# Broadcasting rows with matmuls over all 128 rows of the array

## The reference, cut to what matters

```python
# forgetting attention (8 heads, layer 0 of the first block)
logits = q_b @ k.T * scale + F_b[..., :, None] - F[..., None, :]      # F = cumsum(log_f)
# mLSTM (4 heads, layer 1 of the first block)
D = b[..., :, None] - b[..., None, :] + i[..., None, :]               # decay, then exp
# head norms (second block, both layers), per head of 64 or 32 features
q_gqa = rms_norm_2(q_g.reshape(b, l, GQA_HEADS, GQA_DIM), lp["g_qn_gqa"])
```

## Time and profile before

| | us |
|---|---|
| median of 3 runs | 2605.84 (2600.36 to 2607.82) |
| the profiled execution, its own time | 2602.29 |
| its span | 2600.5 |
| PE busy (matmul records) | 2534.8 (97%) |
| VectorE busy | 1263.5 (49%) |
| ScalarE busy | 534.0 (21%) |
| GpSimd busy | 641.8 (25%) |
| mean granted TensorE clock | 0.983 of full speed |

### The profile page before, as it was taken

The page is one execution under the profiler, slowest core; times in us unless marked ns, Lnnn a source line. Parts: engine busy times, 40 slices in busy tenths (PEclk is TensorE's granted clock), DMA queues, the critical chain, the costliest instruction groups (busy, mean ns, idle before and its releaser), DMA issues.

```text
span 2600.5 us, 36667 instructions
## 1 busy us (share of the span) xinstructions
PE 2534.8 (97%) x14020; PEld 2055.5 (79%) x14020; DVE 1263.5 (49%) x2507; ACT 534.0 (21%) x1167; POOL 641.8 (25%) x523
## 2 busy tenths in 40 slices
PE   8999999999999999999999999999999999999999
PEld 5857889986699998645567767888888865899999
DVE  3024168751325886314646763544552235335774
ACT  1131122111212221212530002222200124212220
POOL 0010134200212530001422321332340004332562
PEclk9989999999899999998999999999999998999999
DMA  6322255644234566110023571222212220243442
GB/s 239 130 97 89 106 208 189 255 174 161 83 130 164 197 230 231 70 59 25 1 81 146 215 270 65 75 88 97 98 68 77 98 83 1 98 171 142 165 179 106
DMA packets 39826, 335.31 MB, mean 129 GB/s; under 512 B 3856, under 2 KB 10128, under 8 KB 22416
## 3 DMA queue, kind: packets, MB, share of 16 engines
q1 hardware_dynamic: 39696, 333.50, 34.6%
HBM read 332.44 MB, written 1.05 MB: 128 GB/s over the span
## 4 chain that ended last, share of the span: by engine, by line
PE 87%; DVE 5%; DMA 3%; issue 2%; POOL 2%; ACT 1%; DVEq 0%; SPq 0%; POOLq 0%; ACTq 0%
PE PS L757 23%; PE PS L557 20%; PE PS L2674 6%; PE PS L1509 5%; PE PS L1019 5%; PE PS L1692 4%; PE PS L1327 3%; PE PS L2715 3%; PE PS L1680 2%; DMA slot<-in_weights 2%; PE PS L2250 2%; PE PS L1338 2%; PE PS L1350 2%; PE PS L432 1%; PE PS L2367 1%
## 5 line engine op out<-in xcount | busy, mean ns | idle before, releaser
L557 PE MATMUL PS<-XN,slot 128*128 128x256 f32 (+1 forms) x1184 | 296.8, 411 | 0.8 <-DVE XN L496 0.8
L757 PE MATMUL PS<-SQ,slot 128*128 128x128 f32 (+1 forms) x1984 | 294.4, 301 | 2.4 <-DVE slot L853 2.4
L757 PEld LDWEIGHTS PS<-SQ,slot 128*128 128x128 f32 x1984 | 268.1, 191 | 15.6 <-DVE slot L853 2.7
L557 PEld LDWEIGHTS PS<-XN,slot 128*128 128x128 f32 x1184 | 224.4, 190 | 69.9 <-issue 42.5
L757 PE MATMUL PS<-XN,slot 128*128 128x128 f32 (+1 forms) x1664 | 250.0, 301 | 0.0
L557 PE MATMUL PS<-arena,slot 128*128 128x256 f32 x1088 | 238.4, 381 | 9.6 <-DMA slot<-in_weights 9.6
L557 PEld LDWEIGHTS PS<-arena,slot 128*128 128x128 f32 x1088 | 208.0, 191 | 38.5 <-issue 9.8
L757 PEld LDWEIGHTS PS<-XN,slot 128*128 128x128 f32 x1664 | 226.1, 192 | 10.7
L880 DVE SCALAR_TENSOR_TENSOR arena<-PS,small,arena 128x255 f32<-128x255 f32 (+2 forms) x352 | 174.8, 543 | 45.9 <-ACT arena L824 45.6
L824 ACT ACTIVATE arena<-PS,small 128x256 f32<-128x256 f32 (+1 forms) x176 | 105.3, 616 | 379.1 <-DVE PS L913 240.4
L1468 POOL TENSOR_SCALAR probs<-probs,pair_rec 128x512 f32<-128x512 f32 (+2 forms) x64 | 88.2, 1383 | 247.7 <-DVE pair_rec L1436 247.7
(11 more groups left out here) (280 smaller groups left out, 3806.0 us busy)
## 6 DMA issues: line engine op xcount, KB each, us to landing
slot<-in_weights SPq DMA_DIRECT2D x85, 2048.0 KB, 7.7
arena<-in_mod SPq DMA_DIRECT2D x96, 512.0 KB, 3.4
slot<-in_weights SPq DMA_DIRECT2D x16, 2816.0 KB, 9.8
slot<-in_weights SPq DMA_DIRECT2D x24, 1536.0 KB, 6.8
slot<-in_weights SPq DMA_DIRECT2D x6, 1024.0 KB, 4.8
slot<-in_weights SPq DMA_DIRECT2D x2, 2176.0 KB, 8.9
arena<-in_c SPq DMA_DIRECT2D x3, 1024.0 KB, 10.4
small<-in_small SPq DMA_DIRECT2D x1, 2685.0 KB, 18.6
```

Of the source, the lines that this page charges most:

```text
L557: mm = pe.matmul(o, l, r, start=k == 0, stop=k == len(terms) - 1, skip_group_check=True)
L757: mm = pe.matmul(PS[:, bank, 0:h], lhs[:, k * P:(k + 1) * P], rhs(k), start=first and k == 0, stop=last and k == 3, skip_group_check=True)
```

## The change

1. `select` now gives one column of the whole 128 x 128 identity, broadcast to as many columns as wanted, and the moving side is all 128 partitions of the row's area (`row_of`). Only the wanted partition meets a 1; the other 127 meet zeros and must only hold finite numbers.
2. In the mLSTM layer a GpSimd memset clears the 128 x 256 area first, and DVE waits for it before it writes the decay rows.
3. A spread of the head norms is 2 matmuls (heads of 64) or 4 (heads of 32), each with 128 rows and 64 or 32 columns of the array, written to its own PSUM partitions. 17 matmuls a layer become 42. The two 0/1 tables leave the table `small` (768 of its columns).
4. Layer 1 of the second block sets 2 x 32 partitions of the unused half of PSUM bank 7 to 1.0 with DVE, and the statistics' matmuls wait for it.

```diff
-        def select(n, h):
+        def select(h, each=P):
-            return ident[0:n, h:h + 1].broadcast_to([n, P])
+            return ident[:, h:h + 1].broadcast_to([P, each])
+        row_of = lambda r: arena[:, 14336 + r * T:14336 + r * T + T]
...
-                        sc.append((i, c0, c1, select(8, 2 * t + i), rows[0:8, 0, 0:c1 - c0], False, True))
+                        sc.append((i, c0, c1, select(2 * t + i), row_of(0)[:, 0:c1 - c0], False, True))
...
-                    dec.append((c0, c1, select(4, h), rows[0:4, 2, 0:n], True, True))
+                    dec.append((c0, c1, select(h), row_of(2)[:, 0:n], True, True))
...
-                add(tensor=tensor_lstm_gates, vector=vector_lstm_gates)
+                add(tensor=tensor_lstm_gates, vector=vector_lstm_gates,
+                    gpsimd=lambda p: p.memset(row_of(2), 0.0).then_inc(*tick(GD, "lstm", "cleared")))
...
                     dve.wait_ge(*of("lstm", "F"))
+                    dve.wait_ge(*of("lstm", "cleared"))
...
+                if nq < 512:
+                    for g in (1, 2):
+                        op = dve.memset(PS[32 * g:32 * g + 32, 7, nq:512], 1.0)
+                    op.then_inc(*tick(VD, hn, "unused_set"))
...
                 claim(pe, STAT)
+                if nq < 512:
+                    pe.wait_ge(*of(hn, "unused_set"))
...
-                lhs, r = sel_rows(name, t)
+                g, _, _, _, heads, _, _, _ = tiles[name, t]
+                each = P // heads
                 claim(pe, bank)
                 pe.wait_ge(*of(hn, "rstd"))
-                pe.matmul(PS[:, bank, 0:n], lhs, RST[r, 0:n], start=True, stop=True)\
-                    .then_inc(*tick(TD, hn, "spread", name, t))
+                for i in range(heads):
+                    mm = pe.matmul(PS[each * i:each * (i + 1), bank, 0:n], select(32 * g + heads * t + i, each), RST[:, 0:n],
+                                   start=True, stop=True, skip_group_check=True)
+                mm.then_inc(*tick(TD, hn, "spread", name, t))
```

More of the change, by code:

```diff
@@ L165, in small_columns @@
     sizes["stat"] = 2
-    sizes["spread_halves"] = 4 * P
-    sizes["spread_quarters"] = 2 * P
     sizes["rope_mla"] = 2 * T
@@ L2387, in scalar_low, with vector_low @@
                     act.activation(q_sq[h], q_dst[h], ACT.Square).then_inc(*tick(SD, hn, "sq", "Q", h))
-            def vector_low(dve, s=s, nq=nq, q_dst=q_dst):
+            def vector_low(dve, s=s, l=l, nq=nq, q_dst=q_dst, hn=hn):
+                if nq < 512:
+                    for g in (1, 2):
+                        op = dve.memset(PS[32 * g:32 * g + 32, 7, nq:512], 1.0)
+                    op.then_inc(*tick(VD, hn, "unused_set"))
                 for m in range(0, 4, 2):
@@ L2416, in two_blocks, with tensor_stat @@
                     stat_groups[g].insert(0, (pick("all", 1), SQ_KR, 512, (f"kv{l}", "read", 2, 0)))
-            def tensor_stat(pe, hn=hn, stat_groups=stat_groups):
+            def tensor_stat(pe, hn=hn, stat_groups=stat_groups, nq=nq):
                 claim(pe, STAT)
+                if nq < 512:
+                    pe.wait_ge(*of(hn, "unused_set"))
                 for i in range(7):
@@ L2470, in two_blocks, with tensor_spread @@
             SIN = [SQ[:, 4 + i, 0:T] for i in range(4)]
[L2472 to L2477, removed]
+            def tensor_spread(pe, name, t, hn=hn, tiles=tiles, bank_of=bank_of):
                 bank = bank_of["S", name, t]
                 n = tiles[name, t][3]
-                lhs, r = sel_rows(name, t)
+                g, _, _, _, heads, _, _, _ = tiles[name, t]
+                each = P // heads
                 claim(pe, bank)
                 pe.wait_ge(*of(hn, "rstd"))
-                pe.matmul(PS[:, bank, 0:n], lhs, RST[r, 0:n], start=True, stop=True)\
-                    .then_inc(*tick(TD, hn, "spread", name, t))
+                for i in range(heads):
+                    mm = pe.matmul(PS[each * i:each * (i + 1), bank, 0:n], select(32 * g + heads * t + i, each), RST[:, 0:n],
+                                   start=True, stop=True, skip_group_check=True)
+                mm.then_inc(*tick(TD, hn, "spread", name, t))
                 lend(bank, (hn, "out", name, t))
@@ L3140, in small_array @@
     put("stat", stat)
-    r, c = i[:, None] % 32, np.arange(4 * P)[None]
-    put("spread_halves", (c // 64 == r) * 1.0)
-    put("spread_quarters", (c[:, :2 * P] // 32 == r) * 1.0)
     i = np.arange(P)
```

## The result

The changed kernel takes **2581.5 us** (median of 4 runs, 2580.5 to 2584.2), the kernel before on the same chip 2606.8 us (4 runs, 2600.4 to 2607.9). The ratio is 0.991, 95% interval 0.9891 to 0.9928: by it the kernel is some 23 us or 0.9% faster (the two medians lie 25.3 us apart). The profiled execution took 2581.9 us (span 2580.1, mean granted clock 0.996), that of before 2602.3 (2600.5, 0.983).

The account below looks back on a forecast made before the run. It took PE's own time, columns and clock, as the bound. Gains 7.7 + 5.9 + 0.3 + 10.4 = 24.3 us bring the profiled 2602.3 to 2578.0; with 3.5 added, median 2581.5 us, range 2572 to 2602.

Parts of the forecast that it names:

- What lets the clock fall: All four places, 71 us at 0.50: matmuls using 4 or 8 rows count little for the clock, full ones count.
- Rival A: All places: clock ignores rows used and falls in the same places; 10.7 us slower, 2616.5 us; chance 8%.
- C: Both head norms: clock kept only where no wait stands before, so it still falls there; 2 us gained, 2604; chance 7%.
- D: One of the four places: clock still falls there, 6 to 10 us of gain missing, 2589 in the middle; chance 14%.
- Forgetting attention: Forgetting attention: 2.75 us a unit, unit 4 starting 13.2 us after unit 0's start instead of 20.9; gain 7.7 us.
- mLSTM: mLSTM layer: four units 7.8 us instead of 12.1, gain 4.3; the records behind them gain 1.6; together 5.9 us.
- Layer 0: Layer 0 head norms: spreads stage 27.5 us instead of 21.8, loss 5.7; scores gain 3.9, Fourier records 2.1; net gain 0.3.
- the change of parting: Switching how the array is parted: 0.1 us a change, ends zero and 0.2; 12 changes, 1.2 us, in each head-norm layer.
- Layer 1: Layer 1 head norms: spreads stage 15.1 us instead of 20.0, gain 4.9; scores 3.9, Fourier records 1.6; gain 10.4 us.
- Memsets and table: mLSTM and layer 1 memsets, and the table smaller by 393 KB: zero effect, at most about 1 us.
- rival B: Head norms: column parts of a spread run one after another; 12.5 us slower, 2618.3 us; chance 3%.
- 3.5 us: Whole run: median of the runs shown lies this far above the profiled execution, so 2578.0 becomes a median of 2581.5 us.

Follow-up runs that it names:

- e5_rows72: Kernel before, with the row-broadcasting matmuls of forgetting attention and mLSTM on 72 of 128 rows, head norms unchanged: 2599.1 us, one run.
- e6_rows32: Kernel before, with the row-broadcasting matmuls of forgetting attention and mLSTM on all 32 rows of a strip, head norms unchanged: 2598.4 us, one run.
- e9_first3r8: Changed kernel, but the first three sets of spreads in both head norms side by side with 8 rows: 2578.9 us, ratio 0.9904 to before.
- e3_spreads: Kernel before, with only the new head-norm spreads on 128 rows in both layers, tables kept: 2596.8 us, ratio 0.997 to before.
- e4_side32: Changed kernel, but head-norm spreads side by side as before, with all 32 rows of their strips: 2585.4 us, ratio 0.9915 to before.
- e1_fox: Kernel before, with only the forgetting attention's selecting matmuls on 128 rows: 2597.2 us, ratio 0.9964 to before.
- e8_first3: Changed kernel, but the first three sets of spreads in both head norms side by side in 32-row strips: 2577.4 us, ratio 0.9897 to before.
- e12_last3: Changed kernel, but the last three sets of spreads in both head norms side by side in 32-row strips: 2591.5 us, ratio 0.9949 to before.
- e2_lstm: Kernel before, with only the mLSTM decay matmuls on 128 rows, plus memset and DVE's wait: 2601.3 us, ratio 0.9984 to before.

## Why the prediction was right, point by point

The forecast was that the clock, not the columns, is what the change buys, and that all four stretches at 0.50 go. They did. By its own terms:

- **What lets the clock fall.** Forecast: few rows count little. Shown, by e5_rows72, e6_rows32 and e9_first3r8, with the addition that the neighbours' rows count with them. In e5_rows72 PE is busy 19.50 of 19.50 us and stays at 0.50, and the change of rows alone takes the stretch away. The rule that the Trainium skill gives in "TensorE: Matmul & The Clock Gate", Part 1 (how busy PE has been) has no place for rows, and the traces do not agree with it. Rival A is out. So are C and D: layer 1's spreads start behind a wait of 1.25 us and stay at 1.00.
- **Forgetting attention**, 7.7 us: measured 7.8; the unit is 2.75 us as priced. The 2.83 us that I read for the old unit "at full clock" hold 0.2 us at half: the clock fell at 160.7, before the last selecting record was through. In e3_spreads, where it fell later, the old unit takes 2.74. The wait of 0.4 to 0.8 us for the probabilities is 0.24.
- **mLSTM**, 4.3 + 1.6: measured 3.7 + 1.6. I had priced a unit at 1.35 us of PE and 0.81 of wait for DVE. The starts stand 2.28 to 2.36 apart, so PE's part is 1.5, but 1.38 in the last unit, behind which PE does not wait. I read the difference of some 0.15 us as the end of the last record, which a next one hides only when PE need not wait; no run tests this.
- **Layer 0**, loss 5.7, gain 6.0: measured 6.7 and 5.9. The mis-sized term is the change of parting. The 17 spreads took 15.8 us, 1.2 more than 17 x 0.86, and the records beside them are longer too: seven rotations took 3.6 us where I had 3.0, three Fourier steps 8.2 where I had 7.8. That is 2.1 us in all over the 12 changes that I had counted, so 0.18 for one in place of 0.1, within the ends that I gave (zero and 0.2). I had also counted too few: the first two sets, which mix spreads of two and of four parts, take 0.27 us more than their columns, the next three 0.14. The part beside the spreads shows in the rows: four Fourier records take 0.97 us to the next start behind a set of spreads (1189.06 to 1190.03), and 0.86 behind rotations (1196.12 to 1196.98), which also have 128 rows and 128 columns.

```profile
1189.06 1.13 PE L2517 MATMUL PS<-small,arena 128*128 128x256 f32 x4
1190.03 1.89 PE L2528 MATMUL PS<-small,arena 128*128 128x256 f32 x8
...
1196.12 1.03 PE L2517 MATMUL PS<-small,arena 128*128 128x256 f32 x4
1196.98 1.89 PE L2528 MATMUL PS<-small,arena 128*128 128x256 f32 x8
```

  At the end of layer 0's spreads I had DVE's last product; it is POOL's rotation (0.90 us of wait), of nearly the same length.
- **Layer 1**, 4.9 + 3.9 + 1.6: measured 3.8 + 5.4. The changes again (the rotations took 3.8 for 3.0) and the wait for POOL at the end (0.93 for 0.57).
- **Memsets and table**, zero: the DVE memsets are 0.27 us each in free time, GpSimd's is 0.31 us, the table landed in 17.7 us in place of 18.6, and nobody waited for any of them.
- **Column parts side by side** (rival B): a set of four, two of them with four parts each, takes 3.72 us; one after the other it would need 12 x 0.86 = 10.3. The Trainium skill, "TensorE: Matmul & The Clock Gate", Part 3 (row and column tiling), has column tiles run concurrently too; the trace agrees.

That the forecast of 2581.5 us was met to a tenth is luck; the total is nearer than its terms. The terms sum to 24.3 us and the places gave 21.5, less 1.1 elsewhere; the profiled execution was to take 2578.0 and took 2581.9. Then I added 3.5 us because the median of before lies that far above its profiled execution; after's median lies 0.4 below its own. The two errors, 3.9 one way and 3.9 the other, cancel. The 3.5 was no property of the kernel but of the one execution that was profiled.

What stays open: how rows count in detail. In all new matmuls the identity column is zero in 127 of the 128 rows. In the attention and the head norms the moving rows that meet these zeros hold other numbers. In the mLSTM they are zeros too, from the memset, in 124 of the rows, and the clock is 1.00 there with 128 rows (and with 72, of which 68 are zeros) where 4 rows let it fall. So rows that only multiply zeros by zeros counted there. Whether they count as much as rows with numbers was not tried. Outside a strip no run has fewer than 72 rows, so between 8 and 64 the number was tried only inside strips. And the fast ends of e4_side32's and e1_fox's runs have no trace behind them.

## What to carry to other kernels

When a long stretch of a busy PE stands at half clock, look at the shapes in its rows before looking for waits: here the same work with 128 rows for 4 or 8, with zeros in all but one row of the stationary side, ran at full clock and gained 23 us though it lost the side-by-side packing. How many rows are enough depended on the neighbours: 72 were between 128-row matmuls and were not between 64-row ones. Pad rows where a thin group stands just before or in a dense one, and keep the packing where enough full work follows; the version that does both (e8_first3) has a stage 5 us shorter than the change's. And read the difference between a profiled execution and the median of its kernel as noise of that execution, not as a term to carry over.

## What the runs showed of the hardware

- A stretch can be busy 19.50 of 19.50 us and stay at 0.50, with 72-row and 64-row matmuls (e5_rows72), while a stretch of 8.30 us with 72-row and 128-row ones, of which PE is busy only 5.88, is at 1.00 (same run).
- The effect is local: the same 17 spreads, with the thin ones first, left the clock at 1.00 (e8_first3, layer 0), and with the thin ones last brought 13.7 us at half clock (e12_last3). In layer 1 the thin ones in front still brought 3.4 us of it (e8_first3).
- At full clock rows cost no time: a side-by-side set is 1.07 us with 8 rows and with 32 (1185.53 to 1186.60 in e8_first3). The attention's four selecting records over 256 columns take 1.05 us from start to start with 8 rows (e3_spreads, below) and 1.06 with 128 (160.25 to 161.31 after). Only the clock tells them apart.

```profile
158.77 0.49 PE L1332 MATMUL PS<-arena 64*128 64x128 f32 x4 [0.99 <-ACT arena L1531]
...
160.46 1.12 PE L1332 MATMUL PS<-arena,small 8*128 8x256 f32 x4
161.51 0.49 PE L1332 MATMUL PS<-arena 64*128 64x128 f32 x4
```

- A row that multiplies zeros by zeros counts for the clock: the mLSTM's 128-row matmuls, zero on both sides in 124 rows, hold it at 1.00 (e2_lstm, where nothing else is changed) and the 4-row ones let it fall to 0.50.
- A change between full matmuls and ones that use a part of the array cost some 0.18 us (estimate: 2.1 us over 12 changes in layer 0, both sides of each counted; two changes between kinds of parts are in it too).
